# Two-layer block on one core: first expert group's gather and gate product by halves; feed forward with high and low rows in one product

## What is computed

```python
def expert_block(args):            # per block of tokens of one expert
    xb, e = args
    hdn = jax.nn.silu(xb @ w1[e]) * (xb @ w3[e])      # gate product, up product
    return hdn @ w2[e]                                # down product

# second block
xn = _rmsnorm(x, ffn_norm[l])
up = xn @ w_up[l]                                     # 1024 x 6144
g_ffn = _causal_dwconv(up[..., :D_FF], ffn_conv_w[l], ffn_conv_b[l])   # 3 taps
x = x + (jax.nn.gelu(g_ffn) * up[..., D_FF:]) @ w_down[l]
g_ple = jax.nn.sigmoid(_rmsnorm(x, ple_norm[l]) @ w_ple_gate[l])
x = x + g_ple * (p[l] @ w_ple_proj[l])
```

## Time and profile before

| | us |
|---|---|
| median of 3 runs (lowest, highest) | 1736.12 (1735.61, 1736.60) |
| the profiled execution | 1736.04 |
| its span in the profile | 1734.3 |
| PE busy in the span | 1363.6 |
| POOL busy | 609.2 |
| ACT busy | 429.1 |
| DVE busy | 423.0 |
| read from HBM | 537 MB, 310 GB/s over the span |

### The profile page before, as it was taken

One profiled execution on the slowest core, in us unless ns is written; L12 is line 12 of the kernel. 1 busy time (PEld: TensorE's weight loads), 2 busy tenths in 40 slices (PEclk: granted clock), 3 DMA queues, 4 the chain that ended last, 5 costly groups with the idle time before them and its releaser, 6 DMA issues.

```text
span 1734.3 us, 21607 instructions
## 1 busy us (share of the span) xinstructions
PE 1363.6 (79%) x9196; PEld 983.1 (57%) x9196; DVE 423.0 (24%) x901; ACT 429.1 (25%) x542; POOL 609.2 (35%) x485
## 2 busy tenths in 40 slices
PE   7999998677557746675666576657799999899998
PEld 7899996333123313331333133222699988899986
DVE  3995554000000000000000000000416642233203
ACT  4444741000000000000000000000547563544434
POOL 6886790000000000000000000000587958688894
PEclk9999999888788878877888788778899999999999
DMA  9453477999999999999999999999445444455551
GB/s 366 147 192 108 176 270 293 384 428 428 427 429 428 428 429 428 429 429 429 429 428 428 429 428 429 429 428 419 164 167 209 156 161 146 146 195 187 176 192 54
DMA packets 46058, 539.56 MB, mean 311 GB/s; under 512 B 4440, under 2 KB 8544, under 8 KB 14624
## 3 DMA queue, kind: packets, MB, share of 16 engines
q1 hardware_dynamic: 42704, 532.44, 75.5%
q0 software_dynamic: 1184, 3.94, 0.6%
q10 hardware_dynamic: 2096, 2.11, 0.4%
HBM read 537.41 MB, written 1.06 MB: 310 GB/s over the span
## 4 chain that ended last, share of the span: by engine, by line
PE 64%; DMA 30%; DVE 2%; SPq 1%; ACT 1%; issue 1%; POOL 1%; DVEq 0%; ACTq 0%
PE bank L595 38%; DMA ring<-in_w 18%; PE bank L823 13%; DMA slab<-in_w 10%; PE bank L808 6%; PE bank L880 2%; DMA ring<-in_units 1%; SPq L408 1%; PE bank L869 1%; POOL ring_parts L533 1%; ACT ring_parts L1107 0%; PE bank L1035 0%; PE bank L989 0%; PE bank L729 0%; PE bank L835 0%
## 5 line engine op out<-in xcount | busy, mean ns | idle before, releaser
L533 POOL TENSOR_TENSOR ring_parts<-ring,ring_parts 128x512 fp32r<-128x512 f32 x448 | 594.6, 1366 | 1007.2 <-ACT ring_parts L1107 1007.1
L595 PE MATMUL bank<-slab_parts,ring_parts 128*128 128x256 f32 x3328 | 498.2, 285 | 2.1 <-DVE rows_parts L1968 2.1
L595 PEld LDWEIGHTS bank<-slab_parts,ring_parts 128*128 128x128 f32 x3328 | 458.1, 193 | 4.4 <-issue 3.1
L823 PE MATMUL bank<-ring,slab 128*32 128x512 f32 x1472 | 254.9, 674 | 168.6 <-DMA slab<-in_w 88.1
L823 PEld LDWEIGHTS bank<-ring,slab 128*32 128x32 f32 x1472 | 68.4, 122 | 340.8 <-issue 339.1
L1107 ACT ACTIVATE ring_parts<-ring 128x2048 fp32r<-128x2048 f32 x114 | 212.0, 1910 | 169.5 <-PE bank L595 167.2
L869 PE MATMUL bank<-ring,slab 128*32 128x512 f32 x752 | 139.2, 724 | 140.5 <-DMA slab<-in_w 70.5
L595 PE MATMUL bank<-rows_parts,ring_parts 128*128 128x256 f32 x752 | 187.2, 286 | 0.0
L869 PEld LDWEIGHTS bank<-ring,slab 128*32 128x32 f32 x752 | 37.4, 130 | 226.1 <-issue 225.4
L595 PE MATMUL bank<-ring_parts,slab_parts 128*128 128x512 f32 (+1 forms) x672 | 160.5, 388 | 3.9 <-POOL ring_parts L533 2.8
L1868 DVE TENSOR_TENSOR slab<-slab,bank 128x512 f32<-128x512 f32 x16 | 11.0, 687 | 578.7 <-PE bank L823 578.7
(11 more groups left out here) (302 smaller groups left out, 941.5 us busy)
## 6 DMA issues: line engine op xcount, KB each, us to landing
ring<-in_w SPq DMA_DIRECT2D x143, 2048.0 KB, 19.8
ring<-in_units SPq DMA_DIRECT2D x59, 2048.0 KB, 8.4
slab<-in_w SPq DMA_DIRECT2D x49, 2048.0 KB, 25.3
ring<-in_units SPq DMA_DIRECT2D x2, 1024.0 KB, 9.2
slab<-bias_scratch ACTq DMA_DIRECT2D x2, 1024.0 KB, 8.6
slab<-in_xT SPq DMA_DIRECT2D x1, 1024.0 KB, 5.0
rows<-in_ln_g POOLq DMA_DIRECT2D x2, 512.0 KB, 17.9
slab<-in_x SPq DMA_DIRECT2D x1, 1024.0 KB, 5.3
```

The lines of the kernel that those rows point to most:

```text
L533: ins = g.tensor_tensor(r32(w_q), w_q, r32(high_q), ALU.subtract)
L595: return mm(out_, l, r, start=start and first, stop=stop and last)
L823: last = mm(b[CAP * j:CAP * j + CAP, :], xg[:, c, CAP * j:CAP * j + CAP], wt[j][:, c, :], start=c == 0, stop=c == DC - 1, tile_position=(0 ...
```

## The change

Part one, group 0 of the experts: the gather is cut in two. Chunks 0 to 3 are gathered, ACT copies them as soon as they are there, and quarters 0 and 1 of the gate product run; then chunks 4 to 7 are gathered, DVE copies them, and quarters 2 and 3 run. The up product of group 0 comes ahead of the gather of group 1. The other groups are unchanged.

Part two, the gate and up units of the feed forward: the low part of the normalized tokens moves to `slab` part 9, and one product takes 512 columns, 256 of high and 256 of low tokens, with the high weights as the stationary side; the low weights then take 256 columns of high tokens. So 8 products of 512 and 8 of 256 stand for 24 of 256. The right half of a bank now holds the high x low sum, and each 128 channels have a bank of their own, four banks for a unit. ACT copies the right half to `slab` part 4, DVE adds it to the left half; this is new work. The multiplication, the high copy and the low part go by 128 x 256 instead of 128 x 512, twice as many. ACT's copy of the up unit's high weights stands behind the last `hidden_high` of the unit before, where it stood ahead of both.

```diff
-        n2 += [f"fg{i}_0", f"fg{i}_1", f"fu{i}_0", f"fu{i}_1"]
+        n2 += [f"f{x}{i}_{j}" for x in "gu" for j in range(4)]
...
+        xn3_parts = (chan(0), chan(9))
+        xn3_both = slab[:, 0:10:9, :]
+
+        def right_half(w, j):
+            return slab[:, 4, 1024 * w + T * j:1024 * w + T * j + T]
...
+            def both_parts(w, tasks, arrive=None):
+                high, low, count = w
+                for m, task in enumerate(tasks):
+                    o, cut = take_bank(task), slice(P * m, P * m + P)
+                    for c in range(DC):
+                        if arrive and m == 0 and c in arrive:
+                            arrive[c]()
+                        if m % 2 == 0 and c == 0:
+                            pe.wait_ge(S("high_ready"), count + m // 2 + 1)
+                        mm(o[:].rearrange("p (a t) -> p a t", a=2), r32(high[:, c, cut]),
+                           r32(xn3_both[:, :, T * c:T * c + T]), start=c == 0, stop=c == DC - 1)
+                    for c in range(DC):
+                        if m % 2 == 0 and c == 0:
+                            pe.wait_ge(S("low_ready"), count + m // 2 + 1)
+                        last = mm(o[:, 0:T], r32(low[:, c, cut]), r32(xn3_parts[0][:, c, :]), start=False,
+                                  stop=c == DC - 1, skip_group_check=True)
+                    full(last, task)
...
-            def gather(number):
+            def gather(number, chunks=range(DC)):
...
-                last.then_inc(S("xg_full"), 1)
+                last.then_inc(S("xg_full" if DC - 1 in chunks else "half_gathered"), 1)
...
             def gate_by_quarters():
+                gather(0, range(4))
                 for quarter in range(4):
+                    if quarter == 0:
+                        pe.wait_ge(S("xg0_copied"), 1)
+                    if quarter == 2:
+                        gather(0, range(4, DC))
+                        pe.wait_ge(S("xg1_copied"), 1)
...
-                wait_xg(number)
                 if first:
                     gate_by_quarters()
+                    gate_up(1, 1, 0)
+                    gather(1)
                 else:
+                    wait_xg(number)
                     gate_up(0, 3 * h, 3 * pair + 3 * h // 2)
...
-            def take_xg(number, beside=True):
-                act.wait_ge(S("xg_full"), number + 1)
+            def take_xg(number, beside=True, first=False):
+                if first:
+                    act.wait_ge(S("half_gathered"), 1)
+                else:
+                    act.wait_ge(S("xg_full"), number + 1)
...
             for i in range(6):
-                weights_high(1, f"fg{i + 1}_1" if i < 5 else down[0])
-                wait_read(act, f"fg{i}_0", f"fg{i}_1")
+                for j in range(4):
+                    copy_right(i, 0, j)
+                weights_high(1, f"fg{i + 1}_3" if i < 5 else down[0])
+                wait_read(act, *[f"fg{i}_{j}" for j in range(4)])
                 A(half(5, i % 2), half(5, i % 2), ACT.Gelu_apprx_tanh).then_inc(S("fgelu_ready"), 1)
-                weights_high(1, f"fu{i + 1}_1" if i < 5 else down[1])
...
+                for j in range(4):
+                    copy_right(i, 1, j)
+                    if j:
+                        hidden_high(i, j - 1)
+                hidden_high(i, 3)
+                weights_high(1, f"fu{i + 1}_3" if i < 5 else down[1])
...
+            def add_halves(i, w, j):
+                dve.wait_ge(S("right_copied"), 8 * i + 4 * w + j + 1)
+                o = bank(f"f{'gu'[w]}{i}_{j}")
+                tt(o[:, 0:T], o[:, 0:T], right_half(w, j), ALU.add).then_inc(S("halves_added"), 1)
```

More of the change, by code:

```diff
@@ L133 @@
            "gd1", "gd3", "yb1", "yb3", "mo0_1", "mo1_1"]
-          + [f"f{x}{i}_1" for i in range(6) for x in "gu"]
+          + [f"f{x}{i}_3" for i in range(6) for x in "gu"]
           + ["dn0_1/1", "dn0_1/2", "dn0_1", "dn1_1/1", "dn1_1/2", "dn1_1", "pp1_1", "pg0_1", "pg1_1"])
@@ L799, in _ @@
             pe.wait_ge(S("x1_ready"), 2 * TT)
-            def gather(number):
+            def gather(number, chunks=range(DC)):
                 pe.wait_ge(S("sel_ready"), number + 1)
-                for c in range(DC):
+                for c in chunks:
                     b = (low_bank, high_bank)[c // 4]
@@ L899, in group @@
                     combine(number - 1)
-                if not final:
-                    gather(number + 1)
-                gate_up(1, 3 * h + 1, 3 * pair + (3 * h + 1) // 2)
+                    if not final:
+                        gather(number + 1)
+                    gate_up(1, 3 * h + 1, 3 * pair + (3 * h + 1) // 2)
                 turn_hidden(number)
@@ L909, in _ @@
             pe.wait_ge(S("consts_ready"), CONSTS)
-            gather(0)
             group(0, 0, 0, first=True)
@@ L1046, in _ @@
             for i in range(6):
-                chan_major(unit(1), xn, [f"fg{i}_0", f"fg{i}_1"], arrive=None if i else as_turned("x3"))
-                chan_major(unit(1), xn, [f"fu{i}_0", f"fu{i}_1"])
+                both_parts(unit(1), [f"fg{i}_{j}" for j in range(4)], arrive=None if i else as_turned("x3"))
+                both_parts(unit(1), [f"fu{i}_{j}" for j in range(4)])
             for u in range(2):
@@ L1053, in _ @@
                     if u == 0:
-                        wait_read(pe, *[f"fu{2 * k + i}_{j}" for i in range(2) for j in range(2)])
+                        wait_read(pe, *[f"fu{2 * k + i}_{j}" for i in range(2) for j in range(4)])
                     w = unit(1)
@@ L1239, in _ @@
             wait_read(act, "pos")
-            take_xg(0, beside=False)
+            take_xg(0, beside=False, first=True)
             silu_gate(0)
@@ L1465, in _ @@
             take_turned("x3", [0, 1], "ffn_norm")
-            wait_landed(act, 1, "fg0_1")
+            wait_landed(act, 1, "fg0_3")
             wait_used(act, "mo0_1")
-            weights_high_half(1, "fg0_1", 0)
+            weights_high_half(1, "fg0_3", 0)
             wait_read(act, "mo1_1")
@@ L1474, in _, with copy_right, hidden_high @@
             take_turned("x3", [2, 3], "ffn_norm")
-            weights_high_half(1, "fg0_1", 1)
-            weights_high(1, "fu0_1")
+            weights_high_half(1, "fg0_3", 1)
+            weights_high(1, "fu0_3")
             down = ["dn0_1/1", "dn0_1/2", "dn0_1", "dn1_1/1", "dn1_1/2", "dn1_1"]
+            def copy_right(i, w, j):
+                o = wait_full(act, f"f{'gu'[w]}{i}_{j}")
+                if i:
+                    act.wait_ge(S("halves_added"), 8 * i - 8 + 4 * w + j + 1)
+                A(right_half(w, j), o[:, T:2 * T], ACT.Copy).then_inc(S("right_copied"), 1)
+            def hidden_high(i, j):
+                act.wait_ge(S("hid_made"), 4 * i + j + 1)
+                A(r32(hT[:, 4 * i + j, :]), bank(f"fu{i}_{j}")[:, 0:T], ACT.Copy).then_inc(S("hid_high"), 1)
             for i in range(6):
-                weights_high(1, f"fg{i + 1}_1" if i < 5 else down[0])
-                wait_read(act, f"fg{i}_0", f"fg{i}_1")
+                for j in range(4):
+                    copy_right(i, 0, j)
+                weights_high(1, f"fg{i + 1}_3" if i < 5 else down[0])
+                wait_read(act, *[f"fg{i}_{j}" for j in range(4)])
                 A(half(5, i % 2), half(5, i % 2), ACT.Gelu_apprx_tanh).then_inc(S("fgelu_ready"), 1)
-                weights_high(1, f"fu{i + 1}_1" if i < 5 else down[1])
[L1484 to L1487, removed]
+                for j in range(4):
[4 more added lines that the diff above has]
+                weights_high(1, f"fu{i + 1}_3" if i < 5 else down[1])
             weights_high(1, *down[2:5])
@@ L1959, in low_turned @@
             def low_turned(pre, js, gain, stage):
+                low = xn3_parts[1] if stage == 1 else xn_parts[1]
                 for j in js:
@@ L1967, in low_turned @@
                         c = 4 * k + m
-                        ins = stt(r32(xn_parts[1][:, c, P * t:P * t + P]), o[:, P * m:P * m + P], col(gain, c),
+                        ins = stt(r32(low[:, c, P * t:P * t + P]), o[:, P * m:P * m + P], col(gain, c),
                                   r32(xn_parts[0][:, c, P * t:P * t + P]), ALU.mult, ALU.subtract)
@@ L2140, in _, with gate_conv, hidden_low @@
             low_turned("x3", [2, 3], "ffn_norm", 1)
[L2142 to L2148, removed]
+            def add_halves(i, w, j):
+                dve.wait_ge(S("right_copied"), 8 * i + 4 * w + j + 1)
+                o = bank(f"f{'gu'[w]}{i}_{j}")
+                tt(o[:, 0:T], o[:, 0:T], right_half(w, j), ALU.add).then_inc(S("halves_added"), 1)
+            def gate_conv(i, n):
+                dst = half(5, i % 2)
+                for c in range(4):
+                    add_halves(i, 0, c)
+                for lag in range(FFN_W):
+                    for c in range(4):
+                        o, wc = bank(f"fg{i}_{c}"), col("ffn_w", FFN_W * (4 * i + c) + FFN_W - 1 - lag)
+                        if lag == 0:
```

(24 more changed lines are left out.)

## The result

The changed kernel takes 1834.76 us (median of 4 runs, 1829.13 to 1835.15) against 1736.17 for the kernel before: ratio 1.055, 95% interval 1.053 to 1.057. I had forecast 1726.1. The profiled execution took 1834.81, its span is 1833.0.

A forecast was written before the change was run, and what follows sets the result against it. Transfers were taken to bound the expert stage, with 6.4 us of standstills, and PE the feed forward. 1736.04 - 4.8 (first group) - 5.1 (feed forward) = 1726.1 us, range 1723.5 to 1731.2.

The forecast's parts named there:

- what stands beside PE: Feed forward: ACT's copies, DVE's additions and POOL's low weights stay within their covers, so they cost nothing.
- The 4 us of cover: Feed forward: PE wants the first low half 12.9 us after a unit and gets it at 8.9.
- PE waiting in the feed forward on POOL: Feed forward: listed, with waits on ACT or DVE, as a sign that the prediction is wrong.
- slower rival: Feed forward: DVE's additions slow POOL to 14.1 us a unit, PE waits, 31 us more, 1762; chance 0.07.
- forecast 11.09 us a unit: Feed forward gate and up units: 0.43 us less each, 5.1 us over twelve units.
- the thinnest cover: First down units: PE wants both low halves at 15.4 us, they come at about 14; 1.4 us cover.
- forecast 4.8 us: First expert group: 6.4 us of transfer standstills go, a new one of 1.6 comes; bounds 2.3 to 5.8.
- The standstill at 300 to 304: First group's gate product: the transfer stream loses 2.9 us for lack of a free buffer; this gap goes.
- the one at 318 to 324: Around the first group's up product: the transfer stream loses 3.5 us; this gap goes.
- 1.6 at 305 to 307: First group: PE's added stop issues down matrix 2 later, a new transfer gap of 1.6 us.
- My rival with half clock in the first two quarters: First group's gate product: quarters 0 and 1 take 7.07 us, gain only 2.3, time 1728.6; chance 0.10.
- forecast 298.4: First group: quarters 0 and 1 end and down matrix 1 is issued then, 3.2 us earlier than at 301.64.

The follow-up runs named there:

- own_wait: The changed kernel with one line different: in the feed forward PE waits through the helper for its own low half; 1731.17 us, ratio to the kernel before 0.996.
- own_wait_again: A second profiled execution of the changed kernel whose feed forward wait goes through the helper, nothing else differing; 1728.79 us, where its first profile took 1733.06.
- part one's lower group: The faster cluster of runs of the kernel before with only the first expert group's change; lowest 1732.9 us, six of nine runs, median of all 1733.01.

## Why the prediction was wrong, and where it was right

**The step that failed** is the paragraph on what stands beside PE. It worked out when each low half would be ready against when PE "wants" it, and took for granted that PE's new wait names that half: "PE wants the first low half 11.1 + 1.8 = 12.9 us after and gets it at 8.9". The diff it rests on shows a raw `low_ready` count where the kernel's helper subtracts two. The 4 us of cover were right and count for nothing: by the same timetable the half that PE asked for is wanted a whole unit, 11.1 us, later, so PE asked 7.1 us before it is ready. With the right index the trace of before gives the price: ACT's first half copy ends 1.9 us into the running unit, POOL's half takes 5.0, so PE would stand from 1.8 to 7.2, 5.4 a unit or 65 us in all, and more in the units where ACT's copy is late. Measured were 5.47 and 6.79 us in turn behind a first wait of 7.57, 74 in all; half clock adds 27 (last section), the wide product saves 4, which makes the 98. "PE waiting in the feed forward on POOL" stood among the prediction's signs of being wrong. Its slower rival had the right place, PE's low products waiting for POOL, but the wrong cause, POOL's speed.

**Sizes.** Feed forward: forecast 11.09 us a unit, measured 11.17 with the own wait, a gain of 4.2 us in place of 5.1. The 256 column products keep their 0.120; a wide product takes 0.230 (1.84 for eight), not the 0.2267 of the down units, so it carries 16.7 ns above its columns. By the Trainium skill, "TensorE: Matmul & The Clock Gate", section "Wait — 56ns, not 53.3ns?", with its fixed 2.5 ns a product, the gain would have been 1.0 us; the trace does not bear it out here. That the copies, additions and the later up copy cost nothing was right once PE waits for its own half: even the thinnest cover, forecast at 1.4 us, held.

Part one: forecast 4.8 us, measured 3.1. The steps can be laid beside own_wait_again, whose gather begins at 289.25 like that of the earlier trace rows. Stretches as in the earlier trace rows:

```profile
300.00:302.00 2.00, 1.74 (x8) 1.55 (x7) 0.15 (x1) 0.00 (x0) 0.00 (x0) 1.00 1.01 430
302.00:304.00 2.00, 1.41 (x8) 0.38 (x12) 1.04 (x3) 0.00 (x0) 0.00 (x0) 0.69 1.04 446
304.00:306.00 2.00, 2.00 (x16) 0.57 (x12) 0.00 (x0) 0.00 (x0) 0.00 (x0) 0.50 0.54 229
306.00:308.00 2.00, 2.00 (x24) 0.60 (x20) 0.00 (x0) 0.00 (x1) 0.00 (x0) 0.95 0.66 156
308.00:310.00 2.00, 2.00 (x24) 0.63 (x20) 0.00 (x0) 0.59 (x1) 0.00 (x0) 1.00 0.86 336
...
318.00:320.00 2.00, 2.00 (x10) 2.00 (x10) 0.00 (x0) 0.00 (x0) 0.00 (x0) 1.00 0.97 401
320.00:322.00 2.00, 2.00 (x10) 2.00 (x10) 0.00 (x0) 0.00 (x0) 0.00 (x0) 1.00 1.06 451
```

The standstill at 300 to 304 is gone, the one at 318 to 324 too, and a new one stands at 304 to 310: (199 + 272 + 92) x 2 / 428 = 2.6 us, where I had 1.6 at 305 to 307. The chain shows the longer gate product, beside the earlier trace rows:

```profile
294.09 3.64 PE bank L868 x32
297.73 4.02 PE bank L834 x16
...
302.59 5.34 PE bank L868 x32
307.93 6.87 PE bank L849 x64
```

Quarters 0 and 1 ran at full clock (3.64), which was better than forecast, and quarters 2 and 3 fell into half clock (5.34 in place of 3.54), which I had not foreseen there. My rival with half clock in the first two quarters came in part: four other profiles with the halves have these two at 5.30 to 5.92 us, between 3.54 at full clock and the 7.07 that I priced. The standstills fell by 6.4 - 2.6 = 3.8 us. Of that 3.4 can be seen late in the stage (six transfers are issued at 1115.96, in the kernel before at 1119.32) and 3.2 at the second block, whose dense work begins at 1228.39 against 1231.55. Where the 0.4 between 3.8 and 3.4 went is open.

In the changed kernel's own profile part one gave nothing. Its gather began at 293.85, 4.7 us later than in the earlier trace rows; 0.7 of that had come by 254 us, before anything changed, and the rest in the routing, where the granted clock is 0.50 from 280 to 290 as in the upper profile of own_wait. With one profile of this kernel, and none of part one's lower group, that the change has no share in this is argued from own_wait, the same program but for the one wait, which came in both ways.

Right with the far wait taken out, in own_wait_again: down matrix 1 is issued at 297.79 (forecast 298.4), the four of group 1 from 314.86 on (313.8), the gate product of group 1 begins at 340.19 (340.3), the stream is saturated from 330 on, and the whole second block is shifted, if by less. 1736.0 - 3.1 - 4.2 = 1728.7, and the lowest runs of own_wait are 1727.6 to 1728.8; its median is 1731.17, so the forecast of 1726.1 was some 2.5 to 5 us too low even so.

## What to carry to other kernels

A wait on a counter is part of the cost of a change: when new code waits on an existing counter, check who else adds to it or is left out, and which item the number names. When PE waits for a producer that itself stands idle, look at which item it waits for before asking who is slow. The version with the one line mended is 0.4% faster than the kernel before (interval 0.27 to 0.55%) and is the one to keep.

## What the runs showed of the hardware

The same program ran 4.3 us apart from execution to execution with one visible difference, the place of half clock in 20 us of short products and waits: own_wait took 1733.06 with a granted clock of 0.50 at 280 to 290, and 1728.79 with it at 289 to 293.

Half clock made a long wait dearer than its length. Behind the wait that ends at 1544.21 the granted clock is 0.50 up to 1549.6, and 1.00 from 1549.7 on. Behind each wait of the changed kernel the eight low products took 2.08 us and the eight wide ones 2.38 to 3.41 (2.99 on average over the twelve), against 0.96 and 1.84 at full clock: 2.3 us on top of a wait of 6.2 on average, 27 us in all, more than a quarter of the loss. The Trainium skill, "TensorE: Matmul & The Clock Gate", section "HAM oscillation — how this bites in real kernels", tells of the same, PE starting cold after each wait for data; the rows agree.

A product of 512 columns in fp32r with its own weight load took 0.230 us with the tokens moving, as two pieces from two places, and 0.2267 with the weights moving. I have no cause for the difference.
